# A two-layer decoder trunk on one core: the order of weighing and turning in PE's attention program

## What is computed

```
for each block of queries (qc: plain, qrc: rotated, gc: gates):
    p_cmp = masked_softmax(qc @ k_cmp.T * scale, block ends <= t);  o_cmp = p_cmp @ v_cmp
    p_sel = masked_softmax(qrc @ k_sel.T * scale, causal);          o_sel = p_sel @ v_sel
    p_win = masked_softmax(qrc @ k_win.T * scale, causal);          o_win = p_win @ v_win
    o = gc[0] * o_cmp + gc[1] * o_sel + gc[2] * o_win
return o @ w_o
```

## Time and profile before

| | before |
|---|---|
| median of 3 runs | 2502.52 us (2502.28 to 2502.96) |
| profiled execution: its own time | 2502.55 us |
| profiled execution: span | 2500.7 us |
| mean granted clock of PE | 0.972 |
| PE busy, of the span | 2346.1 us (94%) |
| DVE busy, of the span | 1536.7 us (61%) |
| ACT busy, of the span | 650.3 us (26%) |

### The profile page before, as it was taken

The page is one execution under the profiler, slowest core; times in us unless marked ns, Lnnn a source line. Parts: engine busy times, 40 slices in busy tenths (PEclk is TensorE's granted clock), DMA queues, the critical chain, the costliest instruction groups (busy, mean ns, idle before and its releaser), DMA issues. The chain is left out here.

```text
span 2500.7 us, 43959 instructions
## 1 busy us (share of the span) xinstructions
PE 2346.1 (94%) x17558; PEld 1915.8 (77%) x17558; DVE 1536.7 (61%) x2159; ACT 650.3 (26%) x1252; POOL 498.6 (20%) x334
## 2 busy tenths in 40 slices
PE   7999998997989789999999999999959998999999
PEld 6888886775666578888887888888748787888887
DVE  7656467736777556555575564657557665665645
ACT  3101015524555511010023310102535552200001
POOL 3213031002222232121230221213111102222211
PEclk9999998998999889999999999999969999999999
DMA  4333332431101032333265233323341102333332
GB/s 138 101 93 93 100 99 86 139 99 57 34 25 27 3 101 84 109 88 105 76 199 133 77 110 93 101 84 106 94 114 40 40 1 79 90 101 88 106 88 72
DMA packets 377089, 217.21 MB, mean 87 GB/s; under 512 B 18880, under 2 KB 360832, under 8 KB 376928
## 3 DMA queue, kind: packets, MB, share of 16 engines
q1 hardware_dynamic: 366768, 196.70, 27.7%
q10 hardware_dynamic: 10160, 18.22, 2.1%
HBM read 199.00 MB, written 15.89 MB: 86 GB/s over the span
## 5 line engine op out<-in xcount | busy, mean ns | idle before, releaser
L171 PE MATMUL bank_b<-hhi_b,w_hi_b 128*128 128x512 f32 x872 | 345.4, 396 | 0.0
L173 PE MATMUL bank_b<-hhi_b,w_lo_b 128*128 128x512 f32 x872 | 339.7, 390 | 0.0
L172 PE MATMUL bank_b<-hlo_b,w_hi_b 128*128 128x512 f32 x872 | 339.7, 390 | 0.0
L164 DVE TENSOR_TENSOR w_lo_b<-w_raw,w_hi_b 128x1024 fp32r<-128x1024 f32 (+1 forms) x165 | 289.9, 1757 | 5.7
L171 PE MATMUL bank_a<-hhi_a,w_hi_a 128*128 128x512 f32 x480 | 188.7, 393 | 7.7 <-DVE hlo_a L558 7.7
L171 PEld LDWEIGHTS bank_b<-hhi_b,w_hi_b 128*128 128x128 f32 x872 | 164.0, 188 | 36.7 <-issue 3.2
L172 PEld LDWEIGHTS bank_b<-hlo_b,w_hi_b 128*128 128x128 f32 x872 | 164.0, 188 | 36.4 <-issue 2.9
L173 PEld LDWEIGHTS bank_b<-hhi_b,w_lo_b 128*128 128x128 f32 x872 | 163.9, 188 | 34.5
L172 PE MATMUL bank_a<-hlo_a,w_hi_a 128*128 128x512 f32 x480 | 188.0, 392 | 0.0
L173 PE MATMUL bank_a<-hhi_a,w_lo_a 128*128 128x512 f32 x480 | 187.7, 391 | 0.0
L164 DVE TENSOR_TENSOR w_lo_a<-w_raw,w_hi_a 128x1024 fp32r<-128x1024 f32 (+2 forms) x96 | 158.3, 1649 | 3.3
(11 more groups left out here) (375 smaller groups left out, 4894.6 us busy)
## 6 DMA issues: line engine op xcount, KB each, us to landing
w_raw<-in_ffn_w_gate_dram SPq DMA_DIRECT2D x88, 512.0 KB, 3.9
w_raw<-in_ffn_w_up_dram SPq DMA_DIRECT2D x88, 512.0 KB, 3.9
w_raw<-in_ffn_w_down_dram SPq DMA_DIRECT2D x64, 512.0 KB, 3.7
w_raw<-in_ffn_w_down_dram SPq DMA_DIRECT2D x32, 384.0 KB, 3.2
w_raw<-in_rw_w_rkv_dram SPq DMA_DIRECT2D x24, 512.0 KB, 3.7
w_raw<-in_kv_w_dram SPq DMA_DIRECT2D x12, 512.0 KB, 4.6
w_raw<-in_rw_w_o_dram SPq DMA_DIRECT2D x8, 512.0 KB, 5.0
w_raw<-in_nsa_w_q_dram SPq DMA_DIRECT2D x8, 512.0 KB, 3.8
```

The lines of the kernel that those rows point to most:

```text
L164: nc.vector.tensor_tensor(lo, raw, fp(hi), ALU.subtract).then_inc(s["w_ready"], 1)
L171: nc.tensor.matmul(out, whi, hi, start=first, stop=False)
L172: nc.tensor.matmul(out, whi, lo, start=False, stop=False)
L173: return nc.tensor.matmul(out, wlo, hi, start=False, stop=last)
```

## The change

In PE's loop the special case for `turn` steps goes. In every step but the first, PE now weighs step u-1 before it turns step u.

```diff
@@ -2439,13 +2439,9 @@
                         turn_gates()
                     if i == 0 and u == 1:
                         pe.wait_ge(s["gates"], 2)
-                    if STEPS[u][0] == "turn":
+                    if u:
                         weigh(i, u - 1)
-                        turn(i, u)
-                    else:
-                        turn(i, u)
-                        if u:
-                            weigh(i, u - 1)
+                    turn(i, u)
 
         @block.scalar
         def _(act):
```

## The result

| | before | changed |
|---|---|---|
| median | 2502.74 us (2502.28 to 2503.93, 4 runs) | 2523.5 us (2520.88 to 2526.12, 4 runs) |
| ratio, with its 95% interval | | 1.0083 (1.0071 to 1.0095) |
| profiled execution: own time, span | 2502.55, 2500.7 us | 2520.88, 2519.1 us |

The change makes the kernel 20.8 us slower. The direction was forecast, the size (12.5 us, range to 2522) was not. The runs of the changed kernel also lie 5 us apart, where those of before lay within 1.7 in this set. The profiled one is the fastest of them.

The account below looks back on a forecast made before the run. PE's in-order stream in the attention stage was taken as the bound, nearly without gaps. Exposed copies of 4.3 + 1.9 + 5.2 + 1.0 = 12.4 us on 2502.55 gave 2515.0 us, 0.5% slower, range 2509 to 2522.

Parts of the forecast that it names:

- Term 1: Weighing t=3 in the next head's compressed step: copy exposed 0.31 us in 14 heads, 4.3 us.
- Term 2: Weighing t=3 at each pass end: no scores follow, the whole 0.94 us copy is open, twice, 1.9 us.
- Terms 3 and 4: Weighing the compressed step: 0.87 us exposed in 6 pair-turning heads (5.2 us), 0.12 in 8 others (1.0 us).
- Terms 5 and 6: Weighing t=2 and t=0: copies stay covered; weighing t=1 takes over the wait before t=2's turn: 0.
- Cost (a): Weighings after a wait load weights in the open: 0 to 0.08 us in some 50 places, taken as 0.
- Cost (b): DVE's combine of t=1 may delay the compressed step's maxima some 0.3 us in 14 heads, taken as 0.
- rival C: New waits in PE's attention stage bring one or two more half-clock stretches, 4.3 to 8.6 us: about 2521; chance 0.12.
- The rule that I set beside rival C: A PE that keeps pausing for data falls back to the low clock and starts each burst cold.
- Rival A: Weighing fills PE's hole before turns, chiefly t=2, if t=1's copy precedes t=2's probabilities: 6.6 us faster, 2495.9; chance 0.04.

Follow-up runs that it names:

- e1: The kernel before, with the weighing of t=2 put ahead of the turn in steps t=3 alone: 2511.49 us, ratio 1.0038.
- e2: The kernel before, with the weighing of t=3 put ahead of the turn in the compressed steps alone: 2511.67 us, ratio 1.0034.
- e3: The kernel before, with the weighing put ahead of the turn in steps t=0, 1 and 2 alone: 2500.93 us, ratio 0.9994.
- e4: The changed kernel, with small unread matmuls ahead of copy waits in compressed-step weighings of pair-turning heads and in t=3 weighings: 2517.61 us, ratio 1.0059.
- e6: The kernel before, order kept; in 6 pair-turning heads the compressed step's weighing also waits needlessly for ACT's copy of t=0: 2507.52 us, ratio 1.0015.
- e11: The kernel before, with small unread matmuls at the stage's start, behind the first scores and at the second pass's start: 2502.02 us, ratio 1.0.
- e8: The kernel before, with ACT copying ahead of exponentials in t=1 and t=2, and PE weighing t=1 before turning t=2: 2497.36 us, ratio 0.9981.
- e10: e8 plus small unread matmuls: 22 before the second pass's first turn, 34 before the stage's first scores, 11 behind them: 2499.52 us, ratio 0.9989.

## Why the prediction was wrong

- **What bounds it, and the mechanism: right.** The turn of u and the weighing of u-1 wait for the same copy. No hole was filled, the waits before turns became waits before weighings, and each copy lost one weighing of cover.
- **Term 1 (weigh t=3): mis-sized.** 0.31 forecast, 0.43 measured in e1: 6.0 us for 4.3. The wait itself was right: from the turn of t=3 to the next turn e1 takes 2009.49 to 2011.32 = 1.83, and I had 0.90 + 0.94. What I had put at nothing is the piece ahead of it: the weighing of t=2 takes 1.38 from its start to that of a turn behind it (2008.11 to 2009.49), and 1.26 where scores follow. Why it does is not shown.
- **Term 2 (pass end):** 0.94 forecast, 1.12 measured: 2.2 us for 1.9. Here that weighing takes 1.36, and from the turn to the next weighing it is 2092.75 to 2094.67 = 1.92, for my 1.84.
- **Terms 3 and 4 (compressed step):** 0.87 and 0.12 forecast, 0.96 and 0.23 in e2: 7.6 us for 6.2. In the changed kernel, with term 1 in the same head, the two together come to 1.30 and 0.57.
- **Terms 5 and 6, at nothing: right** (e3).
- **The sum:** 14.6 us without the clock, 2.2 above mine. Cost (a), restart, is 0.1 a place at most: in the changed kernel the weighing of t=3 goes on 0.15 after the copy's end (1894.06 to 1894.21), for my 0.05. Where the wait was there before (e3) it costs nothing. Cost (b) did not show in any head's length.
- **The clock is what failed.** I held rival C apart from the forecast, at 0.12, as a case in which the waits happened to bring a stretch. It comes on top, in both profiles of the changed kernel. By subtraction it makes 6 us of the 20.8 (20.8 - 14.6). The two traces have the stage 17.4 and 24.4 longer, so 2.8 and 9.8 above the 14.6, and e4, whose waits are filled, stands 6 to 7 us below the changed kernel by the ratios. The step that misled me was "heads with 1.05 and 0.3 us of waits inside run at 1.00 today": that shows they kept the clock, not by how much. e6 shows that 0.44 us more, in the place where it puts it, takes four of six below it. My price per stretch was too high: 4.3 us, from the longer one at the pass start, which e11 puts at 15.75 - 12.04 = 3.7. In a pair-turning head it is 1.9. A part of the reason is that at half clock PE does not wait for copies that it waits for at the full one (the 1.05 us wait for o_lo is gone in the two slow heads). Two to four at 0.8 to 3.5 us each were in the traces, and the high end of my range took in one. Rival C's own figure, about 2521, came nearest, at a chance of 0.12, and with the wrong parts: fewer stretches at a higher price.
- The rule that I set beside rival C (the Trainium skill, TensorE: Matmul & The Clock Gate, Part 1, on oscillation) agrees with the traces of the changed kernel (0.81 in two heads) and of e6 (0.80 to 0.89 in four); e1's heads, as long and at 1.00, show that not every added wait brings it. I had let the heads at 1.00 of the kernel before speak against it.
- **Rival A** fell as argued, and e8 is faster once ACT's copy stands ahead of its exponentials, which was the condition; how much of that is owed to weighing first no run tells.

## What to carry to other kernels

When two pieces of work on an in-order engine wait for the same event, their order fills no hole; it decides which result gets out first and how much work lies over the step that consumes it. Count for each copy what stands between its producer and its next user, before and after. And where PE idles more in a stretch that runs at full clock, put the loss of the clock into the sum, not beside it: a stretch that is at 1.00 today may be near the point at which it falls. Where the change lies in one stage, compare that stage's length in the traces too, since the rest of a long program can scatter by more than the change is worth.

## What the runs showed that I had not expected

- 0.44 us of needless waiting in each of six heads brought half-clock stretches in four of them, 0.3 to 1.7 us each (e6), while e1's waits, in another place of the same heads, brought none.
- The same program holds a varying number of such stretches: 3.8 us of slow clock in one profile of the changed kernel, 7.8 in another.
- The part of the program that no experiment touches took 2256 to 2262 us from one trace to the next.
- Matmuls whose results nobody reads, in waits of 0.3 and 0.7 us, went with a clock of 1.00 in all pair-turning heads and were worth some 7 us to the changed kernel (1.0087 to 1.0059). At the start of the second pass they freed the head behind them, but in e10 the next head lost more, and the time as a whole did not move clear of its interval.
